# Half of a depthwise convolution moved from VectorE to GpSimd, and attention scores issued two heads at a time

## The reference, cut to what matters

```python
u = h @ w_in
z, xbc, dt_f_raw, dt_b_raw, q, k, v, gate_logits = jnp.split(u, ...)
xbc = silu(centred_depthwise_conv(xbc, conv_w, conv_b))   # 3072 channels, 5 taps, 256 tokens
scores = q @ k.T / 8 - slope * dist                       # 12 heads of 64, masked by a window
p = exp(scores - max(scores)); o = p @ v / sum(p)
```

## Time and profile before

| what | us |
|---|---|
| median of 3 runs | 1511.16 (1505.98 to 1514.08) |
| profiled execution, device time | 1513.4 |
| its span | 1511.6 |
| PE busy | 1440.2 (95%) |
| DVE busy | 784.0 (52%) |
| ACT busy | 567.4 (38%) |
| POOL busy | 63.0 (4%) |

### The profile page before, as it was taken

One profiled execution on the slowest core, in us unless ns is written; L12 is line 12 of the kernel. 1 busy time (PEld: TensorE's weight loads), 2 busy tenths in 40 slices (PEclk: granted clock), 3 DMA queues, 4 the chain that ended last, 5 costly groups with the idle time before them and its releaser, 6 DMA issues. The chain is left out here.

```text
span 1511.6 us, 20258 instructions
## 1 busy us (share of the span) xinstructions
PE 1440.2 (95%) x8684; PEld 1076.4 (71%) x8684; DVE 784.0 (52%) x1043; ACT 567.4 (38%) x789; POOL 63.0 (4%) x79
## 2 busy tenths in 40 slices
PE   6999999999988999999999979999979899999997
PEld 6987785343437788874434349899968799799886
DVE  4645562221228557551222255699878865656545
ACT  3344442111013354321101024488667653344432
POOL 1000000000003000000000010100121100000000
PEclk9999999999999999999999999999988999999999
DMA  8553686999994530379999984533411144445451
GB/s 340 179 211 117 260 332 235 428 428 427 428 427 163 177 158 1 112 306 401 427 427 428 427 344 162 205 112 116 164 56 57 57 153 182 167 151 204 175 189 61
DMA packets 27745, 355.16 MB, mean 235 GB/s; under 512 B 2880, under 2 KB 4928, under 8 KB 5760
## 3 DMA queue, kind: packets, MB, share of 16 engines
q1 hardware_dynamic: 25840, 341.85, 57.1%
q0 software_dynamic: 1808, 11.93, 2.0%
HBM read 352.72 MB, written 1.05 MB: 234 GB/s over the span
## 5 line engine op out<-in xcount | busy, mean ns | idle before, releaser
L2091 DVE TENSOR_TENSOR ring_low<-ring,w_rounded 128x2048 fp32r<-128x2048 f32 (+1 forms) x124 | 290.2, 2344 | 243.1 <-ACT w_rounded L1628 235.1
L1628 ACT ACTIVATE w_rounded<-ring 128x2048 fp32r<-128x2048 f32 (+1 forms) x124 | 235.3, 1900 | 312.7 <-PE ps L850 96.9
L850 PE MATMUL ps<-split,w_rounded 128*128 128x256 f32 x960 | 228.9, 286 | 17.8 <-DVE ring_low L2091 16.8
L850 PE MATMUL ps<-split,ring_low 128*128 128x256 f32 x736 | 209.4, 285 | 0.0
L850 PEld LDWEIGHTS ps<-split,w_rounded 128*128 128x128 f32 x960 | 168.4, 192 | 19.4 <-issue 16.8
L850 PE MATMUL ps<-hT_low,w_rounded 128*128 128x256 f32 x512 | 145.1, 283 | 0.0
L850 PEld LDWEIGHTS ps<-split,ring_low 128*128 128x128 f32 x736 | 141.0, 192 | 0.0
L880 PE MATMUL ps<-w_rounded,split 128*128 128x512 f32 (+1 forms) x352 | 125.3, 397 | 3.2 <-DVE split L2914 1.5
L2384 DVE TENSOR_SCALAR split<-ps,work 128x1024 fp32r<-128x1024 f32 x14 | 18.0, 1284 | 197.6 <-PE ps L1150 197.6
L1118 PE MATMUL ps<-work 128*64 128x512 f32 x448 | 100.9, 596 | 4.5 <-DMA work<-experts_w 4.5
L880 PE MATMUL ps<-ring_low,split 128*128 128x512 f32 (+1 forms) x256 | 99.5, 389 | 0.0
(11 more groups left out here) (371 smaller groups left out, 2489.4 us busy)
## 6 DMA issues: line engine op xcount, KB each, us to landing
ring<-slabs SPq DMA_DIRECT2D x65, 2048.0 KB, 8.4
work<-experts_w SPq DMA_DIRECT2D x48, 2048.0 KB, 20.4
ring<-experts_w SPq DMA_DIRECT2D x36, 2048.0 KB, 17.0
w_plain<-experts_w SPq DMA_DIRECT2D x12, 2048.0 KB, 16.8
gb<-ln_gb POOLq DMA_DIRECT2D x6, 1024.0 KB, 9.1
ring<-slabs SPq DMA_DIRECT2D x2, 1024.0 KB, 9.0
hT<-x_feat SPq DMA_DIRECT2D x1, 1024.0 KB, 5.2
work<-c_ret POOLq DMA_DIRECT2D x1, 1024.0 KB, 11.8
```

The source lines that it names most:

```text
L850: last = nc.tensor.matmul(dst[:, at:at + T], w3[a][:, k, c * P:(c + 1) * P], src[b][:, k, :], start=(k == 0 and t == 0), stop=(k == KC - 1 ...
L1628: nc.scalar.activation(rounded_half(q), half_of(ring, q), ACT.Copy).then_inc(w_high, 1)
L2091: V.tensor_tensor(half_of(ring_low, q), half_of(ring, q), rounded_half(q).bitcast(F32), ALU.subtract).then_inc(w_low, 1)
```

## The change

Four things change:

- DVE's `conv(n)` keeps only group `2n`: one tensor_scalar and four scalar_tensor_tensor, each linked to the one before.
- GpSimd does group `2n + 1` for all twelve `n`, in one loop ahead of its state-space work. Each tap after the first is a tensor_scalar into a small buffer `c_tap`, and then a tensor_tensor that adds it to the sum. It signals `conv_odd_ready`.
- ACT's `conv_out` waits for both signals, and so does its copy into `c_raw` from the third slab on.
- `att_scores(c)` computes the heads `2c` and `2c + 1` together, alternating between them matmul by matmul. It is issued in even steps only, and the first pair ahead of both first halves of the projection. `att_bank` is renumbered for it.

Some semaphores of GpSimd's clearing work are merged into one counter (`pool_filled`).

```diff
@@ GpSimd
+            link = chain(pool, pool_chain)
+            for n in range(ATT_H):
+                if n % 2 == 0:
+                    wait_pair_out(pool, PJ["att"] + n // 2)
+                if n >= 2:
+                    pool.wait_ge(xbc_ready, n - 1)
+                ch, acc = 2 * n + 1, c_acc[:, n % 2, 1, :]
+                for k in range(TAPS):
+                    tap = conv_w[:, ch * TAPS + k:ch * TAPS + k + 1]
+                    src = c_raw[:, n // 2 % 2, 2 * (n % 2) + 1, k:k + T]
+                    if k == 0:
+                        last = nc.gpsimd.tensor_scalar(acc, src, tap, None, ALU.mult)
+                    else:
+                        link(nc.gpsimd.tensor_scalar(c_tap[:, k % 2], src, tap, None, ALU.mult))
+                        last = nc.gpsimd.tensor_tensor(acc, acc, c_tap[:, k % 2], ALU.add)
+                last.then_inc(conv_odd_ready, 1)
@@ TensorE
-            def att_scores(hd):
-                s = take_aux(att_bank("scores", hd))
-                half = slice(hd % 2 * DH, hd % 2 * DH + DH)
+            def att_scores(c):
+                s = [take_aux(att_bank("scores", 2 * c + e)) for e in range(2)]
                 for i in range(NT):
-                    last = nc.tensor.matmul(s[:, i * T:(i + 1) * T], a_qkT[half, hd // 2, i * P:(i + 1) * P],
-                                            a_qkT[half, 6 + hd // 2, :], start=True, stop=True)
-                last.then_inc(aux_ready, 1)
+                    for e in range(2):
+                        half = slice(e * DH, e * DH + DH)
+                        last = nc.tensor.matmul(s[e][:, i * T:(i + 1) * T], a_qkT[half, c, i * P:(i + 1) * P],
+                                                a_qkT[half, 6 + c, :], start=True, stop=True)
+                        if i == NT - 1:
+                            last.then_inc(aux_ready, 1)
...
+            att_scores(0)
             for hd in range(2):
-                att_scores(hd)
                 xbc_half(hd)
...
                 att_transposes(hd)
-                att_scores(hd + 2)
+                if hd % 2 == 0:
+                    att_scores(hd // 2 + 1)
                 att_products(hd)
                 xbc_half(hd + 2)
@@ ScalarE, conv_out and the copy into c_raw
                 act.wait_ge(conv_ready, n + 1)
+                act.wait_ge(conv_odd_ready, n + 1)
@@ VectorE, conv
-                    for c in range(2):
-                        ch = 2 * n + c
...
+                    ch, acc = 2 * n, c_acc[:, n % 2, 0, :]
...
                     if k < TAPS - 1:
                         link(last)
```

More of the change, by code:

```diff
@@ L368, in build @@
         c_acc = w_(2 * 2 * 256).rearrange("p (b c t) -> p b c t", b=2, c=2)
+        c_tap = w_(2 * 256).rearrange("p (b t) -> p b t", b=2)
         assert w_.at <= WORK - 2048
@@ L437, in build @@
         att_lse_ready, att_mix_ready, att_y_ready = (sem(n) for n in ("att_lse_ready", "att_mix_ready", "att_y_ready"))
-        raw_zeroed, conv_ready, xbc_ready = sem("raw_zeroed"), sem("conv_ready"), sem("xbc_ready")
+        conv_ready, conv_odd_ready, xbc_ready = sem("conv_ready"), sem("conv_odd_ready"), sem("xbc_ready")
         xdt_ready, m_ready, diag_done = sem("xdt_ready"), sem("m_ready"), sem("diag_done")
@@ L450, in build @@
         hT_high, f_high, f_low = sem("hT_high"), sem("f_high"), sem("f_low")
-        v_ready = sem("v_ready")
+        pool_filled = sem("pool_filled")
+        FILLED = {"v_ones": 1, "P_zero": 2, "raw_zero": 3}
         mask_ready = sem("mask_ready")
         o_ready = sem("o_ready")
-        p_zeroed = sem("p_zeroed")
         var_ready, tile_done = sem("var_ready"), sem("tile_done")
@@ L529, in build @@
                   for layer in range(2)]
-        dve_stats = sem("dve_stats")
         dve_chain = sem("dve_chain")
@@ L575, in att_bank @@
         def att_bank(name, hd):
-            b = {"scores": 3 * hd - 3 if hd >= 2 else hd, "P": 3 * hd + 2 if hd <= 10 else 3 * hd,
-                 "o": 3 * hd + 4 if hd <= 10 else 3 * hd + 2}[name]
+            if name == "scores":
+                b = hd if hd < 2 else 3 * (hd - hd % 2) - 3 + hd % 2
+            elif hd < ATT_H - 2:
+                b = 2 + 3 * (hd - hd % 2) + {"P": (0, 4), "o": (3, 5)}[name][hd % 2]
+            else:
+                b = 2 + 3 * (ATT_H - 2) + {"P": 0, "o": 2}[name] + hd % 2
             return AX["att"] + b
@@ L767, in _ @@
             nc.gpsimd.memset(n_hid_rows, 0.0)
-            nc.gpsimd.memset(n_vcmp[0:CMP_N, :, DH:DH + 1], 1.0).then_inc(v_ready, 1)
-            nc.gpsimd.memset(n_P, 0.0).then_inc(p_zeroed, 1)
+            nc.gpsimd.memset(n_vcmp[0:CMP_N, :, DH:DH + 1], 1.0).then_inc(pool_filled, 1)
+            nc.gpsimd.memset(n_P, 0.0).then_inc(pool_filled, 1)
             fold_norm(1)
@@ L780, in _ @@
             pool.wait_ge(x_plain, 2)
-            nc.gpsimd.memset(c_raw, 0.0).then_inc(raw_zeroed, 1)
+            nc.gpsimd.memset(c_raw, 0.0).then_inc(pool_filled, 1)
             pool.wait_ge(a_ready, 1)
@@ L787, in _ @@
                                       s_a.rearrange("p i (r h) -> p r i h", r=2)).then_inc(copies_ready, 1)
-            nc.gpsimd.memset(s_half, -0.5).then_inc(pool_chain, 1)
+            link = chain(pool, pool_chain)
[10 more added lines that the diff above has]
+                        last = nc.gpsimd.tensor_scalar(acc, src, tap, None, ALU.mult)
+                    else:
+                        link(nc.gpsimd.tensor_scalar(c_tap[:, k % 2], src, tap, None, ALU.mult))
+                        last = nc.gpsimd.tensor_tensor(acc, acc, c_tap[:, k % 2], ALU.add)
+                last.then_inc(conv_odd_ready, 1)
+            link(nc.gpsimd.memset(s_half, -0.5))
             def root(g):
-                pool.wait_ge(pool_chain, 1)
                 wait_aux_out(pool, AX["ssd"] + ssd_bank("squares", g))
@@ L1355, in _ @@
             pe.wait_ge(mask_ready, 1)
-            pe.wait_ge(v_ready, 1)
+            pe.wait_ge(pool_filled, FILLED["v_ones"])
             wait_aux_out(pe, nsa_before("cmp"))
@@ L1817, in _ @@
             act.wait_ge(slab_done, SL["nsa_T"] + 2)
-            act.wait_ge(v_ready, 1)
+            act.wait_ge(pool_filled, FILLED["v_ones"])
             for kv in range(2):
@@ L1833, in _ @@
                                  ACT.Copy).then_inc(aux_out[b % 4], 1)
-            act.wait_ge(p_zeroed, 1)
+            act.wait_ge(pool_filled, FILLED["P_zero"])
             def nsa_exps(u):
@@ L1895, in _ @@
                     nc.scalar.activation(s_A, a_log, ACT.Exp).then_inc(decay_ready, 1)
-            act.wait_ge(raw_zeroed, 1)
+            act.wait_ge(pool_filled, FILLED["raw_zero"])
             def conv_out(n):
                 act.wait_ge(conv_ready, n + 1)
+                act.wait_ge(conv_odd_ready, n + 1)
                 for c in range(2):
@@ L1929, in _ @@
                         act.wait_ge(conv_ready, 2 * (s - 2) + 2)
+                        act.wait_ge(conv_odd_ready, 2 * (s - 2) + 2)
                     nc.scalar.activation(c_raw[:, s % 2, :, 2:2 + T], pair(j).rearrange("p (c t) -> p c t", c=4),
@@ L2672, in conv @@
                 for k in range(TAPS):
-                    for c in range(2):
-                        ch = 2 * n + c
[L2675 to L2681, removed]
+                    ch, acc = 2 * n, c_acc[:, n % 2, 0, :]
+                    tap = conv_w[:, ch * TAPS + k:ch * TAPS + k + 1]
+                    src = c_raw[:, n // 2 % 2, 2 * (n % 2), k:k + T]
+                    if k == 0:
+                        last = V.tensor_scalar(acc, src, tap, None, ALU.mult)
+                    else:
+                        last = V.scalar_tensor_tensor(out=acc, in0=src, scalar=tap, in1=acc, op0=ALU.mult, op1=ALU.add)
                     if k < TAPS - 1:
```

## The result

The changed kernel takes 1527.57 us (median of 3 runs, 1526.91 to 1529.15) against 1511.16 before: a ratio of 1.0119 with a 95% interval of 1.0098 to 1.0140. The forecast of 1506.5 and its range up to 1518 were wrong, in sign too.

What follows compares the result with a forecast made beforehand. PE was taken to set the pace by a hair, with DVE right behind. Scores -5.7, friction between nearly level engines +2.0 and tail -1.0 gave -4.7 us: 1506.5 us at the median, range 1500 to 1518.

Steps and rivals of the forecast that it cites:

- POOL: the step that failed: GpSimd's odd convolution group: five tensor_scalar at 0.40, four adds at 0.60, links at 0.1, together 4.8 us.
- The sum: Whole kernel: -5.7 for scores, +2.0 for friction in the loop, -1.0 in the tail, together -4.7 us.
- Exclusion: Loop step: DVE shuts POOL out of SBUF, 2.1 us by `low` and 1.0 by five convolution instructions.
- PE's 7.86: PE's mean loop step after pairing the scores, 8.33 less 0.47 us.
- The slower rival: DVE's convolution against POOL's taps: whole-instruction exclusion from SBUF makes steps 9.35 or 10.4 us, total 1521 or 1532; chance 0.17.
- Its signs: Slower case: scalar_tensor_tensor median well over 0.48 us, POOL without idle time in the loop, ACT waiting for POOL.
- Scores: PE's score matmuls: two heads overlap in the array's halves, saving 0.84 to 1.05 us a pair, 5.7 in all.
- Cutting PE alone would have stopped after 0.14 us a step.: Loop: DVE is nearly full right behind PE, its work ending 0.14 us before the next step, so both edits are needed.
- The tail: After the loop: PE's 2.1 us wait for `low` shrinks by 1.0 because DVE's last convolutions are shorter.

Runs made afterwards that it cites:

- The probes: Kernel before, with linked GpSimd instructions, four of each kind, added at the end of its queue; one run, 1509.94 us.
- the cheaper form: Changed kernel with GpSimd's tensor_scalar replaced by a tensor_tensor whose second operand is the tap's column broadcast; 1514.88 us, ratio 1.0043.
- paired scores alone: Changed kernel with the whole convolution back on VectorE, keeping only the paired scores; 1506.86 us, ratio 0.9975.
- with pairs and DVE at 8.1: Paired scores, whole convolution on VectorE, transposes and products of two heads paired too; 1505.25 us against 1508.88 before, ratio 0.9978.
- With three taps: Changed kernel with GpSimd doing three of the five taps of the odd groups, the other two left out; 1505.71 us, ratio 0.9971.
- every other odd group, broadcast: Paired scores; GpSimd takes the odd group of every other half only, by broadcast multiplication, VectorE the other 18 groups; 1512.67 us, ratio 1.0023.
- broadcast taps: Changed kernel with GpSimd's tap multiplication as a tensor_tensor with the tap's column broadcast, instead of tensor_scalar; 1514.88 us, ratio 1.0043.

## Why the prediction was wrong

- **POOL: the step that failed.** The sum had "4.8 us, with bounds 4.4 and 5.9" for a group. It is 7.75 undisturbed. A tensor_scalar costs 0.92, not 0.40, and lies outside the bounds of 0.31 and 0.61; five of them make 2.6 of the 2.9 us that were missing. The adds cost 0.74, not 0.60, another 0.6, and the links less than the 0.1 each that I gave them. I had taken the tensor_tensor of the earlier trace rows as a ceiling because it reads twice as much. That reason was never in a row. The probes show one operand with a scalar dearer than two operands (0.92 against 0.74), and the row itself was for a broadcast second operand, which is the cheap form (0.61). The Trainium skill (GPSIMD Engine Reference, section 4.1) calls one-input operations on GpSimd roughly line-rate; the estimate of 0.22 us from its section 3.1 lies four times below the measured 0.92, so for this instruction the measurement decides against it; the copy, 0.40, is nearer to it.
- **Exclusion: there, and less than priced.** I allowed 3.1 us a step; the group above shows 9.59 - 7.75 = 1.8, of which `low` makes 1.5. The true price and this exclusion give 7.75 + 1.8 = 9.6, 1.7 above PE's 7.86 and 1.3 above the 8.33 of before, and POOL's groups do start that far apart.
- **The slower rival had the time and the place, not the mechanism.** It put POOL's group with its waits past 8.33 and 1521 to 1532, and the result is 1527.57. But its mechanism was exclusion for whole instructions at my price; what the runs showed is the price. Its signs all came (scalar_tensor_tensor at a median of 0.58, POOL without idle time, ACT waiting for POOL), so they do not tell a dear instruction from an excluded one; the probes do. Exclusion as a bound appears only with the cheaper form, where DVE and POOL both run without idle time at 8.70.
- **Scores: the overlap right, the saving not.** Eight records take 1.06 us, the full overlap. But "5.7" was mis-sized: paired scores alone shorten the stage by 2.4, of it 1.15 in ten steps. I asked what the scores cost and not what they covered. Between transposes and products they hid ACT's evacuation, and in the odd steps 0.8 of each 1.05 came back as a wait. Pairing transposes and products took the wait away again: 7.7 a step.
- **"Cutting PE alone would have stopped after 0.14 us a step."** The number nearly came true with paired scores alone (8.33 to 8.22), by luck: ACT's evacuation stopped it there. The reason is refuted: with pairs and DVE at 8.1, PE ran at 7.7 for four pairs, and DVE's arrears showed only in the last pair and in the tail (19.6).
- **The tail.** I booked -1.0; tail and the rest up to `ssd` together were +8.7 (4.6 + 4.1). I had said that only POOL's throughput counts and not its delay. At the end of the loop the two are one: POOL works without idle time to 1092.7, so its last two groups start only when the ones before are done, at 1072.46 and 1082.12, and ACT, which waits for them, has the gates' weights queued behind.
- **At the assumed load the total would have come out.** With three taps the group is near the priced one, and the time falls by 4.4 us by the ratio (3.9 between the medians) against the -4.7 of the sum, though by luck, through other terms: 2.4 us of stage from the scores, as with paired scores alone, and 1.6 behind the tail.

## What to carry to other kernels

An operation that an engine has not run in the trace has no ceiling there: a neighbouring operation bounds it only if rows show that the two scale alike, so price it with a probe in the engine's idle time before moving work onto it. Of every instruction that is shortened or moved, ask what waits behind it that it was hiding. Where engines are level within a few per cent, look for arrears at the end of the loop as well as for the pace inside it.

## What the runs showed of the hardware

- GpSimd's tensor_scalar with a column: 0.60, 0.92 and 1.56 us at 128, 256 and 512 columns, 2.5 ns for each further column. With a constant it takes 0.85, and a multiplication by the same column written as a broadcast tensor_tensor 0.61.
- An instruction of GpSimd that meets a 2.28 us subtraction on VectorE waits, in every form that the probes have: their longest are 2.3 to 3.7 us, the copy with its one operand among them (2.34 against 0.40).
- VectorE loses too, and more to the cheaper form: four linked scalar_tensor_tensor take 2.04 us with GpSimd idle (every other odd group, broadcast, at 987.18), 2.60 beside tensor_scalar and adds (the changed kernel), and 3.21 beside broadcast products and adds (broadcast taps). What makes the difference, the form or how closely GpSimd's instructions follow each other, no run here separates.
- PE's granted clock did not follow its busy time over 20 us: in the changed kernel it was 1.00 from 980 to 1000 with PE busy for 16.18 us, 0.94 in the next 20 us with 16.71 and 0.89 in the next with 19.22. Before it was 1.00 in all three, with PE busy throughout.
